# Token norms by halves of 128 tokens, and the last slots before each norm multiplied bank by bank

## The reference, cut to what matters

```python
def first_block(x, ...):
    for l in range(2):                                  # l = 0: _mla, l = 1: _swa
        y = attention(x)
        x = _layernorm(alpha * x + y, ln_mix_g[l], ln_mix_b[l])                              # ln0, ln2
        x = _layernorm(alpha * x + relu2(x @ mlp_w_up[l]) @ mlp_w_down[l], ln_mlp_g[l], ln_mlp_b[l])   # ln1, ln3
    return x

def _layernorm(x, g, b):
    mu = x.mean(-1, keepdims=True)
    var = jnp.square(x - mu).mean(-1, keepdims=True)
    return (x - mu) * lax.rsqrt(var + LN_EPS) * g + b

def second_block(x, mem, ...):
    h = rms_norm(x, norm1_g)                            # rms1
    ...                                                 # RWKV, stick-breaking and memory branches, gates
    x = x + merged @ w_out
    x = x + conv_ffn(rms_norm(x, norm2_g), ...)         # rms2
    return x
```

## Time and profile before

| what | value |
|---|---|
| three runs | 1120.17, 1117.88, 1120.15 us, median 1120.15 |
| profiled execution | 1118.81 us, its span 1117.0 us |
| TensorE busy | 1083.2 us, 97% of the span |
| VectorE busy | 760.6 us, 68% |
| ScalarE busy | 645.0 us, 58% |
| granted TensorE clock | 0.995 of full on the mean |

### The profile page before, as it was taken

The page is one execution under the profiler, slowest core; times in us unless marked ns, Lnnn a source line. Parts: engine busy times, 40 slices in busy tenths (PEclk is TensorE's granted clock), DMA queues, the critical chain, the costliest instruction groups (busy, mean ns, idle before and its releaser), DMA issues.

```text
span 1117.0 us, 22415 instructions
## 1 busy us (share of the span) xinstructions
PE 1083.2 (97%) x8339; PEld 979.8 (88%) x8339; DVE 760.6 (68%) x1300; ACT 645.0 (58%) x1148; POOL 10.0 (1%) x25
## 2 busy tenths in 40 slices
PE   6999999999999899999989999999989999999998
PEld 5978999999887689999989988898889989999997
DVE  5877655557876675555786775636774868877776
ACT  5877555544676765544468753434566447666663
POOL 1000000000000000000000000000000000000000
PEclk9999999999999999999999999999999999999999
DMA  9636656555564356656555332212235664665662
GB/s 348 192 136 208 207 181 185 184 186 188 176 215 135 95 173 186 187 188 188 187 171 169 133 115 77 69 48 77 76 114 170 190 188 124 202 189 184 183 192 94
DMA packets 49170, 181.76 MB, mean 163 GB/s; under 512 B 5536, under 2 KB 5696, under 8 KB 48208
## 3 DMA queue, kind: packets, MB, share of 16 engines
q1 hardware_dynamic: 46512, 168.32, 47.5%
q0 software_dynamic: 1584, 7.63, 2.2%
q10 hardware_dynamic: 1008, 4.89, 1.2%
HBM read 179.74 MB, written 1.07 MB: 162 GB/s over the span
## 4 chain that ended last, share of the span: by engine, by line
PE 85%; DVE 7%; ACT 5%; DMA 2%; issue 1%; DVEq 0%; ACTq 0%; SPq 0%
PE acc L706 27%; PE work L669 12%; PE work L673 12%; PE work L672 12%; PE acc L669 3%; PE acc L672 3%; PE acc L673 3%; ACT whi L1407 1%; DVE wlo L1982 1%; PE work L786 1%; PE work L1167 1%; PE work L1146 1%; DVE res L2005 1%; DMA sqr<-x_t 1%; DMA raw<-weights 1%
## 5 line engine op out<-in xcount | busy, mean ns | idle before, releaser
L1982 DVE TENSOR_TENSOR wlo<-raw,whi 128x1024 fp32r<-128x1024 f32 x319 | 389.0, 1223 | 170.4 <-ACT whi L1407 169.2
L1407 ACT ACTIVATE whi<-raw 128x1024 fp32r<-128x1024 f32 x319 | 335.7, 1056 | 129.1 <-PE acc L706 84.9
L669 PE MATMUL work<-xh,whi 128*128 128x256 f32 x1104 | 314.1, 284 | 5.1 <-DVE xl L1992 4.0
L672 PE MATMUL work<-xl,whi 128*128 128x256 f32 x1104 | 311.6, 282 | 0.0
L673 PE MATMUL work<-xh,wlo 128*128 128x256 f32 x1104 | 311.4, 282 | 0.0
L669 PEld LDWEIGHTS work<-xh,whi 128*128 128x128 f32 x1104 | 209.5, 190 | 14.7 <-issue 4.9
L672 PEld LDWEIGHTS work<-xl,whi 128*128 128x128 f32 x1104 | 209.1, 189 | 3.5
L673 PEld LDWEIGHTS work<-xh,wlo 128*128 128x128 f32 x1104 | 209.8, 190 | 0.0
L706 PE MATMUL acc<-whi,hl 128*128 128x512 f32 x344 | 108.0, 395 | 0.0
L706 PE MATMUL acc<-wlo,hh 128*128 128x512 f32 x344 | 108.0, 395 | 0.0
L706 PE MATMUL acc<-whi,hh 128*128 128x512 f32 x344 | 108.0, 395 | 0.0
(11 more groups left out here) (443 smaller groups left out, 1569.9 us busy)
## 6 DMA issues: line engine op xcount, KB each, us to landing
raw<-weights SPq DMA_DIRECT2D x319, 512.0 KB, 3.6
gb<-ln_rows POOLq DMA_DIRECT2D x4, 1024.0 KB, 6.6
memraw<-mem_t ACTq DMA_DIRECT2D x1, 1024.0 KB, 15.1
x<-mem_tok ACTq DMA_DIRECT2D x1, 1024.0 KB, 18.2
x<-x_tok ACTq DMA_DIRECT2D x1, 1024.0 KB, 8.5
qlat<-bias_scratch POOLq DMA_DIRECT2D x1, 1024.0 KB, 10.7
qlat<-bias_scratch POOLq DMA_DIRECT2D x4, 256.0 KB, 4.4
out_tok<-res SPq DMA_DIRECT2D x4, 256.0 KB, 2.1
```

The lines of the kernel that those rows point to most:

```text
L669: a = mm(dst, whi[:, n % RING, col], hi, start=start, stop=False, skip_group_check=shared)
L672: mm(dst, whi[:, n % RING, col], lo, start=False, stop=False, skip_group_check=shared)
L1407: act_fn(whi[:, n % RING, :], raw[:, n % RING, :], ACT.Copy).then_inc(cut_hi, 1)
L1982: tt(wlo[:, n % RING, :], raw[:, n % RING, :], whi[:, n % RING, :].bitcast(F32), ALU.subtract).then_inc(cut_lo, 1)
```

## The change

1. `last_gathers` multiplies the last two slots of `wo`, of both MLPs and of `out`, and the last one of the sliding-window stage and of the FFN, bank by bank: for a pair, three matmuls of the first slot and three of the second for bank 0, then bank 1, 2 and 3. The slots must all be cut before it begins. For the MLPs the second slot's activations are waited for ahead of its first matmul. `slots_used` is raised for the second slot by its first matmul of the last bank.
2. The norms run by token halves: `mean_of`, `inverse` and `root` work on one half, on columns of one number. VectorE does both banks of half 0, its mean, bank 2, the inverse of half 0, bank 3, and then half 1.
3. `feature_major` turns all eight chunks of half 0 and then those of half 1.
4. The cut that stood ahead of the residual (of the last slot of `wo`, `mlp0`, the sliding-window output, `mlp1`) moves behind the scaling; at ln3 it moves between the inverse of half 1 and the second half's rows.
5. At rms2 there are 6 products of zeros instead of 13.

```diff
+            def last_gathers(stage, parts, second_ready=None):
+                slot_start(parts[-1][0])
+                for t in range(2):
+                    for d in range(2):
+                        for s, (n, hi, lo) in enumerate(parts):
+                            if s and (t, d) == (0, 0) and second_ready:
+                                wait_drained(pe, second_ready)
+                            for a, (left, right) in enumerate(((hi, whi), (hi, wlo), (lo, whi))):
+                                end = s == len(parts) - 1 and a == 2
+                                ins = mm(acc[2 * t + d][:, :], left[:, half(t)], right[:, n % RING, d * 512:d * 512 + 512], start=False, stop=end)
+                                if a == 0 and (t, d) == ((1, 1) if s else (0, 0)):
+                                    ins.then_inc(slots_used, 1)
+                                if end:
+                                    ins.then_inc(sig("acc_full"), 1)
-                for d, t in ((0, 0), (0, 1), (1, 0), (1, 1)):
+                for t, d in ((0, 0), (0, 1), (1, 0), (1, 1)):
...
-                for f in (FC - 2, FC - 1):
-                    down(f, base + FC + f)
+                wait_drained(pe, (stage, FC - 2))
+                last_gathers(stage, [(base + FC + f, hh[:, f % 2, :], hl[:, f % 2, :]) for f in (FC - 2, FC - 1)], (stage, FC - 1))
...
-            feature_major("rms2", 13)
+            feature_major("rms2", 6)
...
+            def root(name, t):
+                act.wait_ge(sig("rinv"), 2 * NORMS[name] + t + 1)
+                act_fn(column("rstd", t), column("var", t), ACT.Sqrt).then_inc(sig("rstd"), 1)
...
             def layer_norm(name, g, b, col, ahead=None, within=None):
-                square_pieces(name, rest, "residual", 4 * NORMS[name])
+                square_pieces(name, rest, "residual", 4 * NORMS[name], range(3))
+                root(name, 0)
+                square_pieces(name, rest, "residual", 4 * NORMS[name], [3])
                 act.wait_ge(sig("shift"), SCALED[name] + 1)
                 act_fn(tok(rest, 0, 1), tok(rest, 0, 1), ACT.Identity, scale=column("rstd", 0), bias=column("shift", 0))\
                     .then_inc(sig("scaled_act"), 1)
+                root(name, 1)
...
-            layer_norm("ln2", "ln_mix_g", "ln_mix_b", 8)
+            layer_norm("ln2", "ln_mix_g", "ln_mix_b", 8, lambda: cuts("swaqo", SWA_SLOT[("w", DC - 1)]))
...
             def layer_norm(name, stage, g, b, col, ahead=None):
-                residual(name, stage)
-                inverse(name, True)
+                residual(name, stage, range(2))
+                mean_of(name, 0)
+                residual(name, stage, [2])
+                inverse(name, 0, True)
+                residual(name, stage, [3])
+                wait_root(name, 0)
                 stt(column("shift", 0), column("mean", 0), -1.0, column("rstd", 0), ALU.mult, ALU.mult).then_inc(sig("shift"), 1)
-                for t, d in ((0, 0), (1, 0), (1, 1)):
-                    ts(tok(rest, t, d), tok(rest, t, d), column("mean", t), column("rstd", t), ALU.subtract, ALU.mult)\
-                        .then_inc(sig("scaled_dve"), 1)
+                mean_of(name, 1)
+                centred_scale(0, 0)
+                inverse(name, 1, True)
+                wait_root(name, 1)
+                centred_scale(1, 0)
+                centred_scale(1, 1)
```

More of the change, by code:

```diff
@@ L1457, in root_table, with square_pieces @@
                 own.link(act_fn(norm_column("table", 1), par[:, 0:1], ACT.Sqrt, scale=0.0))
-            def square_pieces(name, src, ready, done, ahead=None):
-                n = NORMS[name]
-                for q in range(4):
+            def square_pieces(name, src, ready, done, pieces):
+                for q in pieces:
                     t, d = divmod(q, 2)
@@ L1703, in _ @@
             mlp("mlp1", FC)
+            square_pieces("ln3", rest, "residual", 12, range(3))
+            root("ln3", 0)
+            square_pieces("ln3", rest, "residual", 12, [3])
             cuts("mlp1", 2 * FC - 1)
-            def rows_ahead():
-                for j in range(2):
-                    cuts("memkb", j)
-            square_pieces("ln3", rest, "residual", 12, rows_ahead)
+            square_pieces("rms1", x, "x_made", 0, range(2))
+            root("ln3", 1)
             memory_keys("memkb", 0, 1)
-            def keys_ahead():
-                for j in range(1, 3):
-                    memory_keys("memkb", j, j + 1)
-            rms_norm("rms1", "norm1", 0, keys_ahead)
+            root("rms1", 0)
+            square_pieces("rms1", x, "x_made", 0, [2])
+            first_scaled("rms1")
+            square_pieces("rms1", x, "x_made", 0, [3])
+            cuts("memkb", 0)
+            root("rms1", 1)
+            cuts("memkb", 1)
+            for j in range(1, 3):
+                memory_keys("memkb", j, j + 1)
+            rms_chunks("rms1", "norm1")
             cuts("memkb", 2)
@@ L1916, in _ @@
                 cuts("out", j)
-            rms_norm("rms2", "norm2", 4)
+            square_pieces("rms2", x, "x_made", 4, range(3))
+            root("rms2", 0)
+            square_pieces("rms2", x, "x_made", 4, [3])
+            first_scaled("rms2")
+            root("rms2", 1)
+            rms_chunks("rms2", "norm2")
             cuts("out", DC - 1)
@@ L1997, in finish, with residual @@
                 wait_drained(dve, key)
-            def residual(name, stage):
-                for q in range(4):
+            def residual(name, stage, pieces):
+                for q in pieces:
                     t, d = divmod(q, 2)
@@ L2010, in residual, with inverse @@
                 own.link(ts(mean, mean, 1.0 / D, None, ALU.mult))
-                own.link(stt(spare, mean, -1.0, mean, ALU.mult, ALU.mult))
-            def inverse(name, centred):
-                n, spare, squares = NORMS[name], norm_column("spare"), norm_column("square", 4)
-                dve.wait_ge(sig("squared"), 4 * n + 3)
+                own.link(stt(column("spare", t), mean, -1.0, mean, ALU.mult, ALU.mult))
+            def inverse(name, t, centred):
+                n, spare, var = NORMS[name], column("spare", t), column("var", t)
+                dve.wait_ge(sig("squared"), 4 * n + 2 * t + 1)
@@ new lines, in inverse, with wait_root, centred_scale @@
+                dve.wait_ge(sig("squared"), 4 * n + 2 * t + 2)
+                own.link(tt(var, spare, column("square", t, 1), ALU.add))
+                nc.vector.reciprocal(var, var).then_inc(sig("rinv"), 1)
+            def wait_root(name, t):
+                dve.wait_ge(sig("rstd"), 2 * NORMS[name] + t + 1)
+            def centred_scale(t, d):
+                ts(tok(rest, t, d), tok(rest, t, d), column("mean", t), column("rstd", t), ALU.subtract, ALU.mult)\
+                    .then_inc(sig("scaled_dve"), 1)
@@ L2617, in _, with with_output @@
                 cuts("out", j)
-            for q in range(4):
+            def with_output(q):
                 t, d = divmod(q, 2)
@@ L2621, in _ @@
                 tt(tok(x, t, d), tok(x, t, d), acc[q][:, :], ALU.add).then_inc(sig("x_made"), 1)
-            rms_norm("rms2", "norm2")
+            for q in range(3):
+                with_output(q)
+            inverse("rms2", 0, False)
+            with_output(3)
+            wait_root("rms2", 0)
+            rms_scale(0, 0)
+            inverse("rms2", 1, False)
+            wait_root("rms2", 1)
+            rms_scale(1, 0)
+            rms_scale(1, 1)
+            rms_chunks("rms2", "norm2")
             cuts("out", DC - 1)
```

125 lines of the change are left out of this document (75 added, 50 removed).

## The result

The changed kernel takes 1122.86 us (median of 11 runs, 1121.01 to 1123.60) where the kernel before takes 1119.79 us beside it (11 runs, 1117.88 to 1120.54): ratio 1.0032, 95% interval 1.0020 to 1.0043. In a second session the ratio was 1.0034 (1.0022 to 1.0045). So it is slower by 0.3%, 3.1 us by the first medians, where 3.05 was forecast. By the means of both sessions it is 3.4. The profiled execution took 1123.33 us, span 1121.5, mean granted clock 0.992.

A forecast was written before the change was run, and what follows sets the result against it. TensorE, busy 97% of the span, was taken as the bound, with a different bound at each norm. Shifts 0.3 + 1.45 + 0.0 + 2.6 - 0.9 - 0.4 = +3.05 us gave 1122.6 us, range 1119.9 to 1125.2.

The forecast's parts named there:

- ln0, +0.3: At ln0, transposes by token halves make the first chunk 0.43 us later, less 0.13 from the moved cut: +0.3 us.
- ln1, +1.45: At ln1, the same 0.3 us plus a new 1.15 us wait for column 31's activations: +1.45 us.
- ln2, 0.0: At ln2, TensorE's idle time moves from before the transposes to behind them: 0.0 us, range -0.3 to +0.3.
- ln3 and rms1, +2.6: At ln3 and rms1, ScalarE's later squares and cut queue behind half 0's root, delaying the pair: +2.6 us.
- The clock, +0: At rms1, half-clock loss taken as unchanged; full clock would make the place +1.8 us, longer half clock +3.0.
- rms2, -0.9: At rms2, banks closing apart and the halves' chain let the ninth transpose start earlier: -0.9 us.
- the end, -0.4: At the kernel's end, bank order lets the fourth sum start 0.2 us after the last matmul, not 0.6: -0.4 us.
- A: Rival: column 31's stall is absent or hidden, -1.15 us at ln1, sum +1.9 us; chance 0.12.
- B: Rival: rms1 profits from the halves, gaining 1.1 us plus 0.8 of clock, sum -1.45 us; chance 0.10.
- C: Rival: the clock falls more often, at both MLPs' ends or longer at rms1, sum +4 to +5.5 us; chance 0.12.

The follow-up runs named there:

- the third experiment: The changed kernel with the transposes of ln0 and ln1 in the old order: 1120.68 us, ratio 1.0021 to the kernel before.
- The second experiment: The changed kernel with column 30 of both MLPs gathered slot by slot as before, only column 31 bank by bank: 1119.31 us, ratio 1.0008 to the kernel before.
- the sixth experiment: The changed kernel, halves kept, with rms1's squares, cuts and reciprocals in another order on ScalarE and VectorE: 1119.07 us, ratio 1.0002 to the kernel before.
- the fourth experiment: The changed kernel with nine products of zeros between rms1's transpose halves and three ahead of its pair: 1120.49 us, ratio 1.0017 to the kernel before.
- the fifth experiment: The changed kernel with rms2 as one chain for all 256 tokens, transposes in old order: 1122.43 us, ratio 1.0029 to the kernel before.
- the first experiment: The changed kernel with mlp1's last gathers, ln3, rms1 and rms1's transposes as before the change: 1118.36 us, ratio 0.9995 to the kernel before.
- a version of 0.9964 in five runs: The changed kernel with ln3, rms1, mlp1's gathers, mlp0's column 30 and ln0/ln1 transposes as before, plus twelve rms1 zeros: 1114.15 us, then 1115.91 us (0.9980).

## Why the prediction was right, point by point

**ln0, +0.3 (+0.32).** Shown by the third experiment, both parts.

**ln1, +1.45 (+1.62).** The stall was worked out as 1.15 and is 1.15: 1.38 us between two starts that are otherwise 0.23 apart. The table has 0.17 more. 0.11 of it is that the first matmul behind the wait takes 0.34 us to the next and not 0.23, which the sum left out; 0.05 is that the 48 memory products take 5.66 us and not 5.61. The second experiment gives 1.31 for stall and restart, and the third the order.

**ln2, 0.0 (-0.27).** The idle time moved from before the transposes to behind them, as forecast. VectorE took up the first chunk 0.26 earlier than the walk through its list had it; this lies at the end of the stated range.

**ln3 and rms1, +2.6 (+2.39).** The mechanism was that ScalarE's third and fourth squares and the cut queue behind the root of half 0. The 2.43 us of idle ahead of that root and VectorE's two waits on the squares and the cut show it, and the sixth experiment, which reorders just these, takes 1.77 away. The stall at mlp1's end went into the working with only 0.35 us, as VectorE's waits for banks behind an earlier first residual. The rows show 0.17 and 0.20, and VectorE's first residual 2.96 us behind `ha`, where it was 5.09: 2.13 earlier, forecast 2.15. Without the stall, in the second experiment, banks 0 and 1 fill one after the other behind column 30, the first residual stands at 3.27, and the last one at 7.80 as against 7.81. So the stall costs this path nothing. The small rest of the error, 0.24, is there already when VectorE begins the cut behind ScalarE's: 18.26 us behind `ha`, worked out as 18.49.

**The clock, +0 (about +0.5 on the mean).** This is the term that was mis-sized. The prediction left the pair's stretch at half clock as it was and gave it 0.4 more at most. In both profiles of the changed kernel it was longer for the pair: 27 matmuls at 0.21 us in the first (2.55 us lost, before 0.8), and half clock to 593 in the second, with the pair starting at 590.1. Before, the slow stretch began with the transposes (0.50 in the window from 585 on), where it costs little; now the second half's transposes are short and the pair stands behind two waits. That this is why it lies later is argued from the rows, not shown by itself. Over the runs it is less, since the clock falls in other places too: mean clock 0.9946 after (20 runs), 0.9952 before (82 runs of the later sessions), 0.5 us. Table and clock give 3.4, and the means of the runs that stood side by side in the two sessions differ by 3.4 (1122.5 and 1119.2). The Trainium skill's "TensorE: Matmul & The Clock Gate" (Part 1, What's actually happening) has the same rule as in the prediction, that activity releases the clock, and the fourth experiment agrees: zeros in the gaps, full clock.

**rms2, -0.9 (-0.80), and the end, -0.4 (-0.36).** Right; of the first, the fifth experiment gives 0.37 to the banks and 0.43 to the halves, which the prediction hadn't parted.

**The rivals.** A (no stall) fell with the row at 285.23. B (rms1 profits) fell with the table. Even with the other order on ScalarE and VectorE the halves are 0.6 slower than the whole norm, where B had them 1.1 faster. C was half true: the stretches were more and longer in the first profile (17.0 against 10.1 us; 10.3 in the second), and one was longer at rms1, as it had named. But at the holes at the MLPs' ends, which it named too, the clock stayed full, and the first experiment has the long stretch at rms1 without halves.

What luck there was lies in the reference and in errors that cancel: the forecast of 1122.6 took the middle of the shown runs, 1119.5, and no clock. The steps sum to 2.9 and not 3.05 because ln1 was put too low and ln2 and rms1 too high, and the clock, put at nothing, gave 0.5. That the medians differ by 3.07 is closer than the working deserves.

## What to carry to other kernels

In this kernel a norm split into halves gained where its own engines end last and have nothing else queued, 0.43 us at rms2, and lost at rms1, where cuts and another norm stand in the same lists: 0.6 even in a better order, 2.4 in the first one. Where products cover the norm's chain (ln0, ln1) the halves had nothing to gain, and turning by halves cost 0.43 there. Before an order by banks is put at the end of a gather, count what the first bank needs against when the last operand is made: the old order had hidden 1.85 us behind twelve matmuls (2.8 us), the new one had three (0.7 us). When a step is sped up or stalled, look for the next wait behind it: here one of two stalls, and the half-clock stretch at 818, cost nothing, because a later wait took them in.

## What the runs showed of the hardware

The granted clock fell to half in one to four places of a profile (1.2 GHz there), and not always in the same ones. In the kernel before they lay behind a wait (3.25 us ahead of 584; 3.30 ahead of 820) and at one place behind none. There TensorE ran, without a gap, 32 matmuls of 64 columns from 741.2 to 744.9, the last four in the first row, and then the clock went down although the engine was busy all the time, as the windows say:

```profile
744.56 0.44 PE L1100 MATMUL work<-stat,kk 64*128 64x64 f32 x4
```

```profile
744.00:745.00 1.00, 1.00 (x11) 0.87 (x9) 0.00 (x0) 0.00 (x0) 0.00 (x0) 1.00 0.00 0
745.00:746.00 1.00, 1.00 (x6) 1.00 (x7) 0.76 (x2) 0.00 (x0) 0.00 (x0) 0.68 0.00 0
746.00:747.00 1.00, 1.00 (x7) 1.00 (x6) 0.00 (x0) 0.00 (x0) 0.00 (x0) 0.50 0.03 8
```

A busy share of 1.00 doesn't show that the clock is safe. Which of these places fall differs from run to run: the same binary ran with mean clocks from 0.994 to 0.998, and 1116.2 to 1119.9 us with them. "TensorE: Matmul & The Clock Gate" of the Trainium skill (Part 1, What's actually happening) says that the count of slow matmuls at a kernel's start varies from run to run of one kernel. It speaks of the start alone; in the middle of this kernel the spread is of the same kind, 0.994 to 0.998.

A change of 0.1% in this kernel is therefore read from steps in a trace, which repeat within 0.06 us, and not from times: a version of 0.9964 in five runs was 0.9980 in twelve.
